# Low parts of token blocks 2 and 3 made in the up stage's first unit, those of 0 and 1 between the last tile's steps

## The reference

```python
h = rmsnorm(x, g_pre_mix);  proj = h @ w_in          # q, k, v of two head groups
mix = concat(global_attention, window_attention) @ w_o
x = x + rmsnorm(mix, g_post_mix)
h = rmsnorm(x, g_pre_ffn)
u = relu(h @ w_ffn_up)                               # 1024 -> 4096
f = (u * u) @ w_ffn_down                             # 4096 -> 1024
x = x + rmsnorm(f, g_post_ffn)
```

## Time and profile before

| | before |
|---|---|
| median of three runs | 2723.7 us (2721.32 to 2725.67) |
| the profiled execution | 2724.54 us |
| its span | 2722.7 us |
| TensorE busy (matmul) | 2599.4 us, 95% |
| VectorE busy | 1908.2 us, 70% |
| ScalarE busy | 1395.2 us, 51% |
| GpSimd busy | 973.3 us, 36% |
| mean granted clock of TensorE | 0.98 |

### The profile page before, as it was taken

How to read it: one execution, slowest core, us unless ns; L and a number is a source line. 1 busy time by engine, 2 the same in 40 slices (tenths; PEclk the granted TensorE clock), 3 DMA queues, 4 the chain that set the end, 5 groups by cost and what they waited for, 6 DMA issues and landing times. The chain is left out here.

```text
span 2722.7 us, 34573 instructions
## 1 busy us (share of the span) xinstructions
PE 2599.4 (95%) x11730; PEld 2099.2 (77%) x11730; DVE 1908.2 (70%) x2469; ACT 1395.2 (51%) x2082; POOL 973.3 (36%) x688
## 2 busy tenths in 40 slices
PE   7999969999999998989997999899999999999998
PEld 5888747777777776978776888778887888888886
DVE  5566569999999976875557877777785344456665
ACT  3333248888888886873344444444444333323431
POOL 1111159898899894430000333233232000000000
PEclk9999979999999998999998999999999999999999
DMA  5333242211222104634753544644455445445555
GB/s 175 108 102 107 83 114 61 48 42 40 68 53 49 32 13 134 181 92 144 213 176 122 164 144 160 228 135 155 144 173 185 153 158 197 143 142 199 202 180 198
DMA packets 290395, 355.09 MB, mean 130 GB/s; under 512 B 53971, under 2 KB 203603, under 8 KB 289212
## 3 DMA queue, kind: packets, MB, share of 16 engines
q1 hardware_dynamic: 271896, 340.05, 40.5%
q10 hardware_dynamic: 18340, 13.03, 1.7%
HBM read 225.65 MB, written 117.85 MB: 126 GB/s over the span
## 5 line engine op out<-in xcount | busy, mean ns | idle before, releaser
L697 POOL TENSOR_TENSOR p_sum<-p_sum,p_hi 128x1024 f32<-128x1024 f32 x160 | 383.5, 2397 | 31.8 <-issue 16.0
L109 PE MATMUL f_pr<-d_w,d_s 128*128 128x512 f32 x896 | 355.6, 397 | 6.8 <-DVE d_s L1943 4.5
L110 PE MATMUL f_pr<-d_w,d_s 128*128 128x512 f32 x896 | 355.0, 396 | 0.0
L111 PE MATMUL f_pr<-d_w,d_s 128*128 128x512 f32 x896 | 354.8, 396 | 0.0
L111 PE MATMUL f_pr<-wide,u_w_lo 128*128 128x512 f32 x896 | 351.0, 392 | 0.0
L776 DVE TENSOR_TENSOR p_lo<-s_ps,p_hi 128x1024 fp32r<-128x1024 f32 x256 | 313.4, 1224 | 39.6 <-ACT s_ps L730 35.2
L729 ACT ACTIVATE p_hi<-s_ps 128x1024 fp32r<-128x1024 f32 x256 | 263.7, 1030 | 127.5 <-PE s_ps L825 127.4
L762 DVE TENSOR_REDUCE part_max<-m_ps 128x1 f32<-128x1024 f32 x251 | 305.5, 1217 | 16.3 <-PE m_ps L807 16.0
L730 ACT ACTIVATE s_ps<-s_ps 128x1024 f32<-128x1024 f32 x256 | 262.1, 1024 | 0.0
L1980 POOL TENSOR_TENSOR d_rstd<-d_var,d_half 128x1 f32<-128x1 f32 x16 | 11.8, 739 | 614.4 <-DVE d_var L2045 614.4
L1936 ACT ACTIVATE d_s<-d_s 128x1024 fp32r<-128x1024 f32 x112 | 118.7, 1060 | 211.3 <-DMA d_s<-act_blocks 210.8
(11 more groups left out here) (239 smaller groups left out, 5911.3 us busy)
## 6 DMA issues: line engine op xcount, KB each, us to landing
d_s<-act_blocks SPq DMA_DIRECT2D x112, 512.0 KB, 4.0
act_blocks<-u_s_out SPq DMA_DIRECT2D x128, 256.0 KB, 6.4
act_blocks<-u_a_sum SPq DMA_DIRECT2D x96, 256.0 KB, 2.4
d_w_raw<-in_w_ffn_down SPq DMA_DIRECT2D x80, 256.0 KB, 3.9
u_w_first<-in_w_ffn_up SPq DMA_DIRECT2D x16, 1024.0 KB, 6.1
u_w_raw<-in_w_ffn_up SPq DMA_DIRECT2D x16, 1024.0 KB, 6.1
d_w_raw<-in_w_ffn_down SPq DMA_DIRECT2D x32, 512.0 KB, 4.6
x_in<-in_x SPq DMA_DIRECT2D x16, 512.0 KB, 4.4
```

The costliest lines, as they stand in the source:

```text
L109: nc.tensor.matmul(out, stat_hi, mov_hi, start=first, stop=False)
L110: nc.tensor.matmul(out, stat_hi, mov_lo, start=False, stop=False)
L111: return nc.tensor.matmul(out, stat_lo, mov_hi, start=False, stop=last)
L697: nc.gpsimd.tensor_tensor(p_sum[:, s], first, p_hi[:, (UNITS * n + u) % SLOTS].bitcast(F32), ALU.add).then_inc(added, 1)
```

## The change

VectorE's order in the mixing stage changes: low part 0 ahead of normalise(15), low part 1 between it and combine(7), and the low parts of blocks 2 and 3 no longer there. They are made in the up stage's first unit, each behind w_low(0, o). The high parts stay where they are. `split_by` becomes two counts, `high_by` and `low_by`; TensorE's waits for t_made in unit 0 begin with product 2 instead of product 4.

```diff
+LOW_AHEAD = 2
@@ mix_heads, VectorE
+            ahead_low(0)
             normalise(NT - 1, 1)
-            ahead_low(0)
+            ahead_low(1)
             combine(NT // 2 - 1)
-            for o in range(1, T_AHEAD):
-                ahead_low(o)
@@ ffn_up
-    def split_by(g, o):
+    def high_by(g, o):
 
         return 7 * g + o + 1 - T_AHEAD
+
+    def low_by(g, o):
+
+        return 7 * g + o + 1 - LOW_AHEAD
@@ ffn_up, VectorE
         def t_low(g, o):
-            dve.wait_ge(t_hi_made, split_by(g, o))
+            at_least(dve, t_hi_made, high_by(g, o))
             nc.vector.tensor_tensor(t_lo[:, o], ...).then_inc(t_made, 1)
...
         for o in range(1, 7):
             w_low(0, o)
-            if o >= T_AHEAD:
+            if o >= LOW_AHEAD:
                 t_low(0, o)
@@ ffn_up, TensorE
             if n % PAIRS == 0:
-                at_least(pe, t_made, split_by(n // PAIRS, o))
+                at_least(pe, t_made, low_by(n // PAIRS, o))
```

## The result

| | before | after |
|---|---|---|
| median | 2723.7 us (20 runs) | 2728.13 us (20 runs) |
| ratio to before | | 1.0016, 95% interval 1.0009 to 1.0023 |
| the profiled execution, its span | 2724.54, 2722.7 us | 2728.44, 2726.6 us |
| TensorE busy | 2599.4 us | 2608.3 us |
| mean granted clock | 0.98 | 0.976 |

The changed kernel is 4.4 us slower by the medians, 2.5 to 6.3 us by the interval; its span is 3.9 us longer. The runs that start from the changed kernel have its numbers, the last of them two more from `w_sums` on.

What follows compares the result with a forecast made beforehand. The prediction took TensorE's matmuls as the bound, VectorE mattering only where TensorE waits. Its terms, -0.22 us (mixing stage's end) and +3.45 us (unit 0), gave +3.2 us on 2723.7, so 2726.9 us, 8-in-10 range 2723.0 to 2730.0.

Steps and rivals of the forecast that it cites:

- The end of the mixing stage: Mixing stage's end: VectorE done 5.7 us sooner, stores landing 0.87 us later, so the stage ends only 0.2 us sooner.
- Unit 0: Up stage's first unit: two low parts added on VectorE, less the idle they fill, make its chain 3.45 us later.
- TensorE in units 1 to 3: Up stage: TensorE's slack of 2.6 us is eaten; it waits about 0.9 us in all by unit 3's start.
- The turn: From token group 0 to 1: the chain's 3.2 us come out in full; TensorE's first wait grows from 2.91 to 5.4.
- rival 4: TensorE's clock at the turn: more slow matmuls behind the last restart add 0.8 to 3.2 us; chance 0.11.
- the loop: Unit 0 to the turn: VectorE and ScalarE wait only for each other, 18.82 us a unit, so no delay vanishes.
- Rival 1: Unit 0 to the turn: TensorE carries the time, the 3.2 us are swallowed, 2723.5 to 2724.4 us; chance 0.11.
- Rival 2: Mixing stage ends with VectorE alone, stores not counting: 5.7 us sooner, 3.45 lost later, 2721.4 us; chance 0.03.
- Rival 3: Up stage units: GpSimd's sums meet VectorE's L1720 in more units, 1.1 us each; four give 2731.3 us; chance 0.05.
- The sum: Whole kernel: -0.22 at the mixing stage's end and +3.45 in unit 0 give +3.2 us, 2726.9 us.

Runs made afterwards that it cites:

- the two delays: Two runs on the kernel before: unit 8's first product made twice on TensorE, 2723.65 us; five sums added on VectorE ahead of w_sums(9), 2730.05 us.
- the order-only kernel: Kernel before with low part 0 ahead of normalise(15), low part 1 ahead of combine(7), low parts 2 and 3 left in the mixing stage; 2723.88 us.
- the kernel with the change and the cut: Changed kernel with ScalarE making the high parts of the next unit's products 5 and 6 ahead of the squares of C22 and C21; 2717.17 us.

## Why the prediction was right, point by point

- **The end of the mixing stage**, -0.22 us: measured -0.19. That two queues' stores, and not VectorE, would set it was right; normalise(15) was 0.85 late (0.87 expected), and VectorE's 5.7 us shrank to 0.2.
- **Unit 0**, +3.45 us: measured +3.79. The term was mis-sized by 0.34 us, the pause ahead of L1724 which no row of before shows. In all five kernels with low parts 2 and 3 in unit 0 the way from w_sums(0) to w_sums(1) is 18.67 or 18.68 us, in the five without 14.87 to 14.89; 3.79 more and not 3.45, so they all have it. What makes it wasn't tried.
- **TensorE in units 1 to 3**: waits of 0.9 us by unit 3 were expected, a little of it at unit 2. The listed waits, 0.41 at unit 1 and 0.45 at unit 3, add up to that, but by luck: by its starts TensorE was 0.40 us late at unit 1, 0.66 at unit 2 and 1.4 at unit 3. Of the 0.5 us that the forecast has too little, 0.34 is the pause.
- **The turn**: the wait for the first low part should have grown to 5.4 us and the restart have come 3.2 us late; it was 5.10 and 3.81, which is 3.2 + 0.29 of the stages ahead + 0.34 of the pause. The wait was shorter than forecast because TensorE itself came later. The sum of the four waits fell, though, from 13.3 to 12.2, where 13.3 + 2.6 was forecast. That step failed, by its own rival 4: the product behind the 5.1 us wait ran at the lower clock and filled 2.2 us of the next wait, and more slow matmuls followed. The time didn't change by it: the loop sets when each wait ends, and from the last wait's end to the span's end it is 944.4 us in both traces.
- **Rival 1**, TensorE carrying the time, fell with the two delays: 2.7 us on TensorE cost nothing, and the 5.0 us by which VectorE's loop was late came out as 5.8 (4.1 to 9.8). The chain of the end changes to TensorE at 1737.68 only because two times lie within 0.06 us of each other.
- **Rival 2** fell with SyncE's drain. **Rival 3** did not occur: w_sums stepped 18.8 us a unit from unit 4 on in group 0, and in group 1 each step is that of before to 0.03 us. Its reading that only units 1 and 2 are hit was too narrow: GpSimd's sums meet VectorE's in the later units too, only other ones (in unit 8 of the kernel before, L1722 took 1.62 us and L1729 1.77), and this is already in the step of 18.8. **Rival 4** had its mechanism right, but the 0.8 to 3.2 us that it named did not come: restarts were slower, and the last wait still ended 3.81 us later and no more.
- **The sum**: +3.2 us forecast, 2726.9; the medians are 4.4 apart (2.5 to 6.3), the traces 3.9, of which 0.29 is from stages ahead. -0.19 + 3.79 = 3.6. The forecast misses by the pause alone; that the medians lie 0.8 us above the traces' 3.6 is within their interval.

## What to carry to other kernels

Where two side engines feed each other in a hand-written order, look at whom they wait for: if the main engine is never the releaser, they keep a time of their own, a delay put on them is kept until the main engine holds them or has to wait for them; here it was kept over 15 units and came out at the turn. In such a stretch a microsecond on the busiest engine can be free and one on an idle-looking engine cost in full; the edit that paid here was not to move work about but to cut the loop's own waits until the main engine was in it. And before an engine's tail is emptied at a stage's end, see who is second: here 5.7 us were bought and 0.2 came.

## What the runs showed of the hardware

VectorE's pause of 0.43 us between two 128x512 sums that stand in the same order in all kernels appears in the five kernels with low parts 2 and 3 in unit 0 and in none of the other five; the profile names no releaser for it. The number of matmuls at the lower clock (granted clock 0.50 from 1446.60 to 1451.40 in the changed kernel) at the up stage's start differs though the engine had been idle equally long. After 11.2 us idle, the matmuls of 0.62 or 0.63 us behind the first were 9 to 12 in six kernels: 11 in the order-only kernel, 12 in the kernel with the change and the cut, and 9 in the changed kernel. After 12.2 us idle they were 6 to 12 in four. The Trainium skill, "TensorE: Matmul & The Clock Gate", Part 1, says that this number varies from run to run of one kernel; no run here has two traces of one kernel, but those that were idle equally long ahead of that point differ.
